# Unread products on TensorE in front of 21 waits of a hybrid decoder step

## The reference, cut to what matters

```python
mod = silu(c) @ ada_w + ada_b                       # 6 vectors of 1024
h = rms_norm(x, norm1_w) * (1 + sc1) + sh1
proj = h @ w_in                                     # 2816 + 8 columns
y_pool = pool_mixer(u_pool)                         # trailing windows 2/4/8/16
q_a, k_a = rms_norm(q_a, q_norm_w), rms_norm(k_a, k_norm_w)
y_att = moba_attention(q_a, [past_k, k_a], [past_v, v_a])   # 8 heads of 64
y_dn  = gated_delta_rule(conv+silu+l2norm of q_d, k_d, v_d) # chunks, triangular solve
x = x + g1 * (concat(y_pool, y_att, y_dn) @ w_out)
h2 = rms_norm(x, norm2_w) * (1 + sc2) + sh2
x = x + g2 * ((silu(h2 @ w_gate) * (h2 @ w_up)) @ w_down)
```

## Time and profile before

| | us |
|---|---|
| median of 3 runs | 626.78 |
| lowest and highest | 626.45, 630.81 |
| profiled execution | 624.19 |
| its span, first to last instruction | 622.3 |
| PE busy in the span | 532.4 (86%) |
| DVE busy | 347.6 (56%) |
| mean granted clock of TensorE | 0.884 of 2.4 GHz |

### The profile page before, as it was taken

How to read it: one execution, slowest core, us unless ns; L and a number is a source line. 1 busy time by engine, 2 the same in 40 slices (tenths; PEclk the granted TensorE clock), 3 DMA queues, 4 the chain that set the end, 5 groups by cost and what they waited for, 6 DMA issues and landing times.

```text
span 622.3 us, 9565 instructions
## 1 busy us (share of the span) xinstructions
PE 532.4 (86%) x3597; PEld 423.2 (68%) x3597; DVE 347.6 (56%) x541; ACT 168.4 (27%) x235; POOL 44.2 (7%) x107
## 2 busy tenths in 40 slices
PE   4759899898999688784839967987999999999997
PEld 2428567575688466453405415966999999999997
DVE  1045275568788776845463256564646646644441
ACT  2310110631132122311000113435343443433331
POOL 7300000000104600000010100000000000000000
PEclk9868969988699879765865778999999999999999
DMA  6995428457049446616446999776564664555201
GB/s 204 300 350 197 125 79 270 129 139 240 0 143 324 151 133 205 206 65 203 135 139 220 322 342 336 234 235 193 181 186 157 201 194 151 181 186 185 71 19 35
DMA packets 99434, 114.63 MB, mean 184 GB/s; under 512 B 7343, under 2 KB 82240, under 8 KB 99372
## 3 DMA queue, kind: packets, MB, share of 16 engines
q1 hardware_dynamic: 93368, 104.46, 52.5%
q10 hardware_dynamic: 5188, 7.67, 3.7%
q0 software_dynamic: 832, 1.89, 0.8%
HBM read 111.20 MB, written 2.97 MB: 183 GB/s over the span
## 4 chain that ended last, share of the span: by engine, by line
PE 67%; DVE 19%; DMA 5%; ACT 4%; issue 3%; SPq 1%; ACTq 1%; DVEq 0%
PE bank L335 63%; DVE prod L896 3%; DVE s_all L992 3%; DVE mats L896 2%; DMA ring<-in_ada_w_dram 2%; DMA ring<-in_w_out_dram 2%; DVE cv L1100 1%; DVE BTP L896 1%; PE bank L504 1%; PE bank L351 1%; PE bank L380 1%; ACT w_part L1683 1%; DMA prod<-in_dn_norm_w_dram 1%; DVE w_ab L896 1%; ACT adaS L1515 0%
## 5 line engine op out<-in xcount | busy, mean ns | idle before, releaser
L335 PE MATMUL bank<-a_hi,w_part 128*128 128x264 f32 x832 | 154.8, 287 | 3.9 <-DVE a_lo L1437 2.1
L896 DVE TENSOR_TENSOR w_part<-ring,w_part 128x2048 fp32r<-128x2048 f32 (+1 forms) x38 | 84.9, 2236 | 89.5 <-ACT w_part L1683 89.5
L335 PEld LDWEIGHTS bank<-a_hi,w_part 128*128 128x128 f32 x832 | 130.9, 191 | 4.7 <-issue 2.6
L335 PE MATMUL bank<-a_lo,w_part 128*128 128x264 f32 x416 | 119.0, 286 | 0.0
L1683 ACT ACTIVATE w_part<-ring 128x2048 fp32r<-128x2048 f32 (+1 forms) x38 | 70.9, 1871 | 86.0 <-PE bank L335 76.2
L335 PE MATMUL bank<-hT,ring 128*128 128x264 f32 x352 | 88.5, 415 | 4.1 <-ACT proj L1538 2.1
L335 PEld LDWEIGHTS bank<-hT,ring 128*128 128x128 f32 x352 | 71.7, 206 | 21.1 <-issue 7.9
L335 PEld LDWEIGHTS bank<-a_lo,w_part 128*128 128x128 f32 x416 | 79.7, 192 | 0.1
L335 PE MATMUL bank<-hid_hi,w_part 128*128 128x264 f32 x352 | 64.9, 285 | 0.0
L335 PEld LDWEIGHTS bank<-hid_hi,w_part 128*128 128x128 f32 x352 | 54.5, 188 | 0.1
L335 PE MATMUL bank<-hid_lo,w_part 128*128 128x264 f32 x176 | 49.7, 282 | 0.0
(11 more groups left out here) (319 smaller groups left out, 588.1 us busy)
## 6 DMA issues: line engine op xcount, KB each, us to landing
ring<-in_ada_w_dram SPq DMA_DIRECT2D x24, 1024.0 KB, 7.4
ring<-in_cache_k_dram SPq DMA_DIRECT2D x64, 256.0 KB, 3.7
ring<-in_w_in_dram SPq DMA_DIRECT2D x11, 1024.0 KB, 5.8
ring<-in_w_gate_dram SPq DMA_DIRECT2D x11, 1024.0 KB, 5.3
ring<-in_w_up_dram SPq DMA_DIRECT2D x11, 1024.0 KB, 5.4
ring<-in_cache_v_dram SPq DMA_DIRECT2D x40, 256.0 KB, 3.8
ring<-in_w_down_dram SPq DMA_DIRECT2D x8, 1024.0 KB, 5.2
ring<-in_cache_v_dram ACTq DMA_DIRECT2D x24, 256.0 KB, 4.1
```

The source lines that it names most:

```text
L335: return pe.matmul(out, lhsT, rhs, start=start, stop=stop, skip_group_check=True)
L896: return v.tensor_tensor(out, a, b_, op)
```

## The change

A helper `keep_awake(b, n)` issues n products of the identity with itself (128x128, 128 columns, float32) into bank b, after a wait for the last reader of that bank. Nobody reads what they write: each later use of the bank starts with a product that overwrites. Such calls stand in front of the wait of 13 places, and `att_turn` gets the same products after its `opened`, which moves ahead of the wait for `probs`. Counts, in the order of execution: QSUM 6, QR 3, QB0 3, QB1 3, DNORM 10, H0 to H7 14, 8, 2, 16, 4, 4, 18, 6 with POOL 8 ahead of H5, OWN 8, DMAX 9, DEXP 5, V0 9, VE 8 and 4, and 12 before the wait for `mix_lo` ahead of the output projection. That is 160 products in front of 21 waits. No other engine's stream changes.

```diff
@@ -334,6 +334,13 @@
             def mm(out, lhsT, rhs, start=True, stop=True):
                 return pe.matmul(out, lhsT, rhs, start=start, stop=stop, skip_group_check=True)
 
+            def keep_awake(b, n):
+
+                if n and frees[b]:
+                    pe.wait_ge(bank_free[b], frees[b])
+                for _ in range(n):
+                    mm(bank[b][:, 0:P], ident[:, :], ident[:, :])
+
 
             pe.wait_ge(sem("ident_made"), 1)
             pe.wait_ge(sem("rows_in"), 16 * 11)
@@ -408,22 +415,25 @@
                     closed(last, f"proj{j}")
                 read_by(f"proj{j}", ("win", item))
 
-            def head_sums(name, ready, src, b_):
-
+            def head_sums(name, ready, src, b_, awake=0):
+
+                keep_awake(b_, awake)
                 pe.wait_ge(sem(ready), 1)
                 b = opened(name, b_)
                 for c in range(AC):
                     last = mm(b[0:2 * AC, 0:NT], headsum[:, c, :], src(c), c == 0, c == AC - 1)
                 closed(last, name)
 
-            def head_spread(name, ready, row, banks):
-
+            def head_spread(name, ready, row, banks, awake=0):
+
+                keep_awake(banks[0], awake)
                 pe.wait_ge(sem(ready), 1)
                 for c in range(AC):
                     b = opened(f"{name}{c}", banks[c % len(banks)])
                     closed(mm(b[:, 0:NT], sel8[:, c, :], rbc[0:2 * AC, row, :]), f"{name}{c}")
 
-            def to_rows8(name, ready, c0, n=1):
+            def to_rows8(name, ready, c0, n=1, awake=0):
+                keep_awake(3, awake)
                 pe.wait_ge(sem(ready), n)
                 b = opened(name, 2)
                 for c in range(AC):
@@ -431,6 +441,7 @@
                 closed(last, name)
 
             def q_spread(b_):
+                keep_awake(3, 3 if b_ < 2 else 0)
                 pe.wait_ge(sem("q_rows8"), 1)
                 b = opened(f"qb{b_}", 2)
                 closed(mm(b[:, :], ident[0:NS, b_:b_ + 1].to_broadcast([NS, P]), nat8[:, 0, :]), f"qb{b_}")
@@ -481,6 +492,7 @@
                     closed(last, f"ctail{hlf}")
 
             def pool_maps():
+                keep_awake(3, 8)
                 pe.wait_ge(sem("pool_diff"), 1)
                 pe.wait_ge(sem("poolw_in"), 16 * 2 * PCH)
                 for c in range(PCH):
@@ -498,8 +510,10 @@
                 closed(mm(b[:, P:3 * P], proj[r:r + 64, QC0 + c, P:T], proj[r:r + 64, KC0 + c, 0:T]), f"S{h}")
 
             def att_turn(h):
+                b = opened(f"PT{h}", h % 2)
+                for _ in range((14, 8, 2, 16, 4, 4, 18, 6)[h]):
+                    mm(b[:, 0:P], ident[:, :], ident[:, :])
                 pe.wait_ge(sem("probs"), h + 1)
-                b = opened(f"PT{h}", h % 2)
                 for n in range(3):
                     last = pe.transpose(b[:, n * P:(n + 1) * P], sm[:, h % 2, n * P:(n + 1) * P], ident[:, :])
                 closed(last, f"PT{h}")
@@ -696,6 +710,7 @@
 
 
             def own_scores():
+                keep_awake(6, 8)
                 pe.wait_ge(sem("own_diag"), 1)
                 b = opened("own", 6)
                 closed(mm(b[:, 0:NS * H], ones[0:NS, :], own8[:, 1, :]), "own")
@@ -708,11 +723,13 @@
                 closed(last, "sT")
 
             def spread_max():
+                keep_awake(5, 9)
                 pe.wait_ge(sem("max_diag"), 1)
                 b = opened("pmax", 5)
                 closed(mm(b[:, :], ones[:, :], w_a[:, :]), "pmax")
 
             def denominators():
+                keep_awake(5, 5)
                 pe.wait_ge(sem("exps"), 1)
                 b = opened("den", 6)
                 closed(mm(b[:, :], ones[:, :], w_b[:, :]), "den")
@@ -730,6 +747,7 @@
 
             def page_values(q):
                 if q == 0:
+                    keep_awake(4, 9)
                     pe.wait_ge(sem("p_ready"), 1)
                 b = opened(f"pv{q}", 4 + q % 2)
                 for hf in range(HALVES):
@@ -745,7 +763,9 @@
                     fold(q - 1)
 
             def page_end():
+                keep_awake(4, 8)
                 closed(fold(NS - 1), "y8")
+                keep_awake(5, 4)
                 pe.wait_ge(sem("y8_out"), 1)
                 b = opened("yT8", 7)
                 for c in range(AC):
@@ -758,13 +778,13 @@
 
             go = {
                 "W": project, "BA": lambda _: decay_inputs(), "CEXT": lambda _: cached_rows(), "A": ada_pair,
-                "QSUM": lambda _: head_sums("qss", "q_sq", lambda c: mixT[:, c, :], 2),
+                "QSUM": lambda _: head_sums("qss", "q_sq", lambda c: mixT[:, c, :], 2, 6),
                 "KSUM": lambda _: head_sums("kss", "k_sq", lambda c: mixT[:, AC + c, :], 2),
                 "DSUM": lambda _: head_sums("dss", "d_sq", lambda c: sq4[:, c, :], 4),
                 "QNORM": lambda _: head_spread("qn", "q_rec", 0, (2, 3)),
                 "KNORM": lambda _: head_spread("kn", "k_rec", 1, (2, 3)),
-                "DNORM": lambda _: head_spread("dn", "d_rec", 2, (4, 5, 6, 7)),
-                "QR": lambda _: to_rows8("q8", "q_done", QC0), "QB": q_spread,
+                "DNORM": lambda _: head_spread("dn", "d_rec", 2, (4, 5, 6, 7), 10),
+                "QR": lambda _: to_rows8("q8", "q_done", QC0, 1, 3), "QB": q_spread,
                 "KR": lambda _: to_rows8("k8", "k_done", KC0),
                 "VR": lambda _: to_rows8("v8", "proj_out", VC0, out_count(VC0 + AC - 1)),
                 "KROW": lambda _: kv_rows("krow", KC0, "k_done", 1),
@@ -801,6 +821,7 @@
                 part_free[item] = (bank_full[b], n)
 
 
+            keep_awake(0, 12)
             pe.wait_ge(sem("mix_lo"), 2)
             def square_sum(c):
                 pe.wait_ge(sem("sq2"), c + 1)
```

## The result

The changed kernel takes 606.39 us (median of 4 runs, 604.71 to 607.08) against 627.83 us before: a ratio of 0.9648, with a 95% interval from 0.9605 to 0.9692. That is 21.4 us or 3.5% less. The forecast was 615.3 us in a range of 605 to 627; its own range began at 609. The sign and the mechanism were right and the size was not: 11.5 us were forecast. The profiled execution took 604.71 us for a span of 603.0 us, so the difference of the spans is 19.3 us.

A forecast was written before the change was run, and what follows sets the result against it. In the middle stage no engine is full: PE and DVE hand work over and PE partly runs at 1.2 GHz. Credit of 12.9 us less 1.4 exposed takes 11.5 off 626.78, giving 615.3 us, range 605 to 627.

The forecast's parts named there:

- Price of one added product: Each added product costs 0.11 us at 2.4 GHz or 0.21 at 1.2 GHz; 160 make 17.6 or 33.6 us.
- Stretches 2, 4 and 6: Slow-clock stretches at H0, H4 and H6 to H7: 7.8 us at most, a third credited, 2.6 us.
- What is exposed: Added products not hidden in waits: DNORM 1.1 us and H5 0.3 us, 1.4 us in all.
- stretches 2 and 3: Slow clock at 214.5 to 224.8 us (H0) and 231.6 to 235.0 us (H1): at most 2.5 and 1.6 us back.
- stretch 5: Slow clock at 269.1 to 279.4 us, from H5 on: at most 4.8 us back, three quarters credited, 3.6 us.
- stretch 1: Slow clock at 78.0 to 88.2 us, behind QNORM and QR: at most 4.4 us back, half credited, 2.2 us.
- stretch 4: Slow clock at 255.5 to 262.3 us, at H4: at most 2.1 us back, credited with a third.
- stretch 7: Denominator and value pages, 316.9 to 340.8 us: at most 4.3 us back, limited by loads; a third credited, 1.4 us.
- The clock stays up throughout: Rival: all 24.4 us come back less 1.4 exposed, 23.0 us off, 603.8 us; chance 0.13 (below 609).
- Overrun: Rival: blocks before ended waits delay what follows, cost 3.5 us, nothing comes back, 630.3 us; chance 0.08 (above 627).
- Patches too thin: Rival: clock falls nearly as before, only stretches 3 and 8 gain, 1.7 us off, 625.1 us; chance 0.24.
- swallowed behind: Rival: gains ahead of 325.93 us end in waits for loads, 624 to 626 us; counted with the thin patches' 0.24.

The follow-up runs named there:

- all_waits: Changed kernel with some counts cut and blocks added in front of waits it had left alone; 593.19 us against 631.57 for the kernel before, ratio 0.9415.
- half: Changed kernel with half of every block's products, 77 instead of 160; 616.82 us against 627.79 for the kernel before, ratio 0.9833.
- after_again: Second profile of the changed kernel, with nothing altered; span 605.2 us.
- tail_only: Changed kernel with only the 55 products from OWN to the output projection kept; 623.50 us, ratio 0.9874 to the kernel before.

## Why the prediction was right, and where its size was off

- *What bounds the kernel.* Right: the middle stage lost 20 us at the same busy time of DVE, and the last one changed by less than 1 us. Without the products nothing changed. Too strong was "the last stage can give nothing": it took 2.9 us less than before in `all_waits`, where two more of its waits were filled.
- *Price of one added product, 0.11 us.* This is one of the two terms that were mis-sized; the other is what the value pages give, below. The rate per instruction was right: 0.11 to 0.12 us at 2.4 GHz, 0.21 at 1.2 GHz. But the row it came from holds eight transposes as eight instructions, while a float32 product is two. The trace of the kernel before had shown it: a `W` stage, told as 16 products, stands in the timeline as 32 (the row below), and the value pages' "16 products" of the earlier trace rows are 8 products of the code. The sum is 35 us at full clock, not 17.6.

```profile
139.13 7.39 PE L335 MATMUL bank<-hT,ring 128*128 128x264 f32 x32
```

- *How much of each wait is filled.* It follows from the price. H6's 18 products were said to leave 3.3 of 5.3 us idle; the trace has 1.06 us. Stretches 2, 4 and 6 were to keep two thirds of their loss: no fall of the clock is left between 170 and 309 us. With half the products, which is the fill that was reckoned with, the total came out near the forecast, 616.8 for 615.3 us. That speaks for the size of the fill, not for each term: the profiled execution of `half` took 624.16 us, so no stage of it can be laid beside the ledger.
- *From which pause on the clock falls.* The prediction took 1.7 us as harmless and 2.2 us as harmful, from one wait each. The length of a wait alone doesn't decide (last section).
- *What is exposed.* DNORM 2.2 us for 1.1, by the same factor. The block before the output projection was put down as covered and ended 0.7 us behind its release, H5's ended 0.6 us behind, and V0's 1.1 us, as it ran at 1.2 GHz. Together 4.6 us for 1.4. That H3's block vanishes in H4's wait was right, though it is twice as long.
- *What a full clock gives back.* The sizes held: 3.9 us from K11 to K12 against 4.1 for stretches 2 and 3, 3.9 against 4.8 for stretch 5, 2.0 against the half of 4.4 for stretch 1, but only 1.0 against 2.1 for stretch 4. Too small was stretch 7, by more than any other term. Its bound came from one row of ten us with a load share of 0.67, but the stretch before it had 0.23 and those behind it 0.95 and 0.86. Value pages that are used up at full clock keep the loads running from the start:

```profile
315.00:325.00 10.00, 10.00 (x106) 5.08 (x104) 7.16 (x15) 0.00 (x0) 0.00 (x0) 1.00 1.00 352
325.00:335.00 10.00, 10.00 (x100) 5.16 (x102) 1.34 (x3) 1.84 (x2) 2.81 (x4) 0.83 1.04 382
```

  At 352 and 382 GB/s the stage from V0 to the output projection took 6.2 us less (4.1 in the second profile), not 3.3 at most. Of the 7.8 us by which the profile's gain is above the forecast's 11.5, this stage has 5.1.
- *The rivals.* "The clock stays up throughout" came nearest, 603.8 for 606.4 us, and the time lies in its range, below 609. It was given 0.13 for want of a reason why the rests should be short, and that reason was the second instruction. That its number is so near is in part luck: the clock did not stay up (0.94 in the stage) and 4.6 us were exposed instead of 1.4, and the value pages, which gave 6.2 us, made up for it. "Overrun" did not decide with full products, though DNORM's block is one, but 8-partition products made it happen: slower than before by 1.8%. "Patches too thin" and "swallowed behind" are refuted, the latter by the stages behind V0, which kept their lead, and by the attention blocks alone, which brought 2.7%. The rule of the Trainium skill ("TensorE: Matmul & The Clock Gate", section "Part 1: The HAM clock gate") that the ramp costs under 1% of a typical kernel does not hold for this one: 3.5% came back.
- *What would show it.* 320 instructions came instead of 160. The clock of the stage went to 0.94 rather than 0.9, and DVE's wait behind DNORM to 3.4 rather than 2.3 us. The last stage's gain of 1.5 us at its start was there, and was lost again in a longer stretch at 1.2 GHz, behind the 4.5 us wait of the last modulation turn that has no block (412 to 419 us):

```profile
412.79 1.09 PE L387 MATMUL bank<-ident,prod 128*128 128x128 f32 x4 [4.49 <-DVE modT L943]
413.53 0.57 PE L335 MATMUL bank<-a_hi,w_part 128*128 128x264 f32 x1
```

## What to carry to other kernels

Where PE's path is cut by waits of 2 to 5 us and its granted clock falls behind them, filling the waits with unread products over all 128 partitions is worth up to half of the PE time on the path that stands at 1.2 GHz; count the matmul instructions that one product makes, and size a block to end just before its release at 2.4 GHz. A block before a wait that has already ended is a plain loss, so take the counts from a trace and take it again when they have changed. Look at the loads behind as well, since a faster PE frees the ring earlier.

## What the runs showed of the hardware that was not expected

- Products on 8 partitions, as many and as long at 2.4 GHz as full ones, left the mean clock at 0.883, and those on 64 partitions raised it to about 0.91 but left the time at 0.995 of the old one, where full ones brought 0.95 and 0.965. What PE does in a wait matters, not only that it is busy. How the gain grows between 64 and 128 partitions was not tried.
- The same wait is followed by a fall of the clock in one execution and not in another. Ahead of W4 PE idles for 2.06 us, with no block there, and the 32 instructions behind it take 9.0 us in the kernel before, 10.4 in `after_again` and 7.4 in `tail_only`, where the clock stays at 2.4 GHz:

```profile
124.63 9.04 PE L335 MATMUL bank<-hT,ring 128*128 128x264 f32 x32 [2.06 <-ACT proj L1538]
```

```profile
125.49 7.36 PE L335 MATMUL bank<-hT,ring 128*128 128x264 f32 x32 [2.06 <-ACT proj L1559]
```

- The clock falls at different places in two executions of one kernel. The profiles of `all_waits` have mean clocks of 0.977 and 0.964, with K6 to K7 at 5.5 in both but K5 to K6 at 21.9 and 23.1 us. So a step of under 1% in the counts can't be judged by the median of a few runs, and the local difference (DNORM's 2.2 us) has to be read in the trace.
